# Gated retention outputs transposed by DMA on SyncE's queue instead of on TensorE

## The reference, cut to what matters

```python
proj = x @ w_in
q, k, v, g, cb, cc, cx, gr, gc = jnp.split(proj, SPLIT_IDX, axis=-1)
o, S = retention(q, k, v, S0, chunk_len)           # o: (B, L, 4 heads, 512), S carried from tile to tile
o = o * lax.rsqrt(jnp.mean(o * o, axis=-1, keepdims=True) + RMS_EPS)   # per-head norm
r = (jax.nn.silu(g) * o).astype(x.dtype) @ w_ret_out                   # 2048 -> 1024
m = jax.nn.sigmoid(gr) * r + jax.nn.sigmoid(gc) * c                    # c: the convolution's branch
h = layer_norm(DEEPNORM_ALPHA * x + m @ w_o, ln1_g, ln1_b)
```

## Time and profile before

| | |
|---|---|
| median of 3 runs | 1608.8 us |
| profiled execution, slowest core | 1608.5 us |
| span from first to last instruction in it | 1607.1 us (cores from 1603.9) |
| TensorE busy | 98% |
| VectorE, ScalarE, GpSimd busy | 50%, 29%, 17% |
| DMA engines: weights' queue, SyncE's queue | 59.2%, 9.2% |

### The profile page before, as it was taken

How to read it: one execution, slowest core, us unless ns; L and a number is a source line. 1 busy time by engine, 2 the same in 40 slices (tenths; PEclk the granted TensorE clock), 3 DMA queues, 4 the chain that set the end, 5 groups by cost and what they waited for, 6 DMA issues and landing times.

```text
span 1607.1 us, 27303 instructions; the slowest of 8 cores (1603.9 to 1607.1 us)
## 1 busy us (share of the span) xinstructions
PE 1570.0 (98%) x9196; PEld 874.3 (54%) x9288; DVE 798.9 (50%) x1469; ACT 468.2 (29%) x923; POOL 271.0 (17%) x504
## 2 busy tenths in 40 slices
PE   5999999999999999999999999999999999999997
PEld 2555566655664455555665566445555566556653
DVE  3566673255222856667424622275666852472226
ACT  1555511113110055552111311005555221131100
POOL 1122211012110322221101211022221110121102
PEclk9999999999999999999999999999999999999998
DMA  9955875569862698587565995369955877578621
GB/s 189 158 80 91 173 109 88 83 121 189 145 99 50 125 198 179 103 200 113 86 96 106 187 147 100 53 132 183 198 118 111 157 138 110 90 136 143 105 41 79
DMA packets 61382, 201.16 MB, mean 125 GB/s; under 512 B 6848, under 2 KB 8512, under 8 KB 61248
## 3 DMA queue, kind: packets, MB, share of 16 engines
q0 software_dynamic: 40752, 149.70, 59.2%
q1 hardware_dynamic: 19920, 48.66, 9.2%
q10 hardware_dynamic: 576, 1.05, 0.3%
HBM read 329.11 MB, written 19.96 MB: 217 GB/s over the span
## 4 chain that ended last, share of the span: by engine, by line
PE 90%; DVE 4%; issue 2%; DMA 2%; POOL 1%; DVEq 0%; ACTq 0%; POOLq 0%
PE P L906 21%; PE P L552 14%; PE P L720 11%; PE P L799 11%; PE P L938 9%; PE P L821 7%; PE P L517 7%; PE P L869 2%; PE P L674 2%; PE P L622 2%; DMA sb_W<-wb 1%; PE P L652 1%; PE P L618 1%; DVE sb_stat L844 1%; POOL sb_stat L848 1%
## 5 line engine op out<-in xcount | busy, mean ns | idle before, releaser
L906 PE MATMUL P<-sb_R,sb_W 128*128 128x384 bf16 x2112 | 345.7, 326 | 0.0
L906 PEld LDWEIGHTS P<-sb_R,sb_W 128*128 128x128 bf16 x2112 | 206.3, 98 | 136.0
L188 POOL DMA_DIRECT2D sb_W<-wb x278 | 153.3, 556 | 753.0 <-PE P L906 278.1
L552 PE MATMUL P<-sb_W,sb_xT 128*128 128x512 bf16 x1119 | 261.4, 379 | 3.1 <-DMA sb_W<-wb 1.0
L720 PE MATMUL P<-sb_xT,sb_W 128*128 128x384 bf16 x1152 | 196.0, 326 | 0.0
L552 PEld LDWEIGHTS P<-sb_W,sb_xT 128*128 128x128 bf16 x1152 | 110.6, 98 | 127.6 <-issue 4.2
L517 PE MATMUL P<-sb_xT,sb_W 128*128 128x384 bf16 x768 | 143.9, 333 | 16.4 <-ACT sb_xT L978 13.5
L720 PEld LDWEIGHTS P<-sb_xT,sb_W 128*128 128x128 bf16 x1152 | 110.9, 98 | 72.1 <-issue 1.2
L814 DVE TENSOR_TENSOR sb_scr<-P,sb_scr 128x384 f32<-128x384 f32 x96 | 53.5, 557 | 191.5 <-PE P L821 161.2
L911 ACT ACTIVATE sb_scr<-P 128x384 f32<-128x384 f32 x132 | 64.7, 490 | 247.9 <-PE P L906 247.9
L799 PE MATMUL P<-sb_xT,sb_W 128*128 128x384 bf16 x768 | 133.1, 326 | 0.0
(11 more groups left out here) (83 smaller groups left out, 1698.3 us busy)
## 6 DMA issues: line engine op xcount, KB each, us to landing
sb_W<-wb POOLq DMA_DIRECT2D x278, 512.0 KB, 10.3
sb_xres<-xp SPq DMA_DIRECT2D x16, 512.0 KB, 12.3
sb_xres<-sret SPq DMA_DIRECT2D x16, 512.0 KB, 15.5
yp<-sb_RA SPq DMA_DIRECT2D x16, 512.0 KB, 3.8
ss_o<-sb_xres SPq DMA_DIRECT2D x16, 512.0 KB, 9.2
sb_lnp<-lnp SPq DMA_DIRECT2D x12, 512.0 KB, 11.1
sb_xT<-xT POOLq DMA_DIRECT2D x5, 768.0 KB, 13.5
sb_cst<-cs SPq DMA_DIRECT2D x6, 384.0 KB, 8.6
```

Source lines behind the costliest of these rows:

```text
L188: self.E[q].dma_start(out=o, in_=i).then_inc(self.dsem[key], 16)
L552: S.pe([(lambda kc=kc: nc.tensor.matmul(P[b][:, :], xtile(s, kc, t), ws[kc // 4][:, kc % 4, :], start=(kc == 0), stop=(kc == 7)), [wc_(s, ...
L906: S.pe([(lambda kc=kc: nc.tensor.matmul(P[b][:, 0:n], w[:, kc, ji * 128:ji * 128 + 128], hT(kc, c0, c0 + n), start=(kc == 0), stop=(kc == 7)),
```

## The change

`og_tr` becomes one DMA transpose on SyncE's queue for each tile, from `og` straight into `goT`. `og` grows from two tiles to a ring of four, in a slot `so` that counts through all tiles of all heads; each slot has a semaphore (`gt0` to `gt3`). ScalarE's squares go into the slot that `gated` will write, so `junk` is gone. The scratch tiles shrink from 512 to 384 columns, the most that is used of them. The keys' transposes stay as they are.

```diff
-    def dma(self, q, key, pairs, reads=(), writes=()):
+    def dma(self, q, key, pairs, reads=(), writes=(), turn=False):
...
-            self.E[q].dma_start(out=o, in_=i).then_inc(self.dsem[key], 16)
+            (self.E[q].dma_start_transpose if turn else self.E[q].dma_start)(out=o, in_=i).then_inc(self.dsem[key], 16)
...
-        SCR = Reg("scr", 4 * 2048)
+        SCR = Reg("scr", 4 * 1536)
...
-        OG_ = Reg("og", 2 * 1024)
-        JK = Reg("junk", 1024)
+        OG_ = Reg("og", 4 * 1024)
...
-            S.op("act", lambda: nc.scalar.activation(out=junk(0), in_=P[b][:, :], func=AF.Square, accum_out=stat[:, c:c + 1]),
-                 reads=[f"P{b}"], writes=[junk.c(), sc(c)])
+            so = (h * NT + t) % 4
+            S.op("act", lambda: nc.scalar.activation(out=og(so), in_=P[b][:, :], func=AF.Square, accum_out=stat[:, c:c + 1]),
+                 reads=[f"P{b}"], writes=[og.c(so), sc(c)])
...
-                S.op("dve", lambda: nc.vector.scalar_tensor_tensor(out=og(t % 2), in0=P[b][:, :], scalar=stat[:, c + 1:c + 2],
+                S.op("dve", lambda: nc.vector.scalar_tensor_tensor(out=og(so), in0=P[b][:, :], scalar=stat[:, c + 1:c + 2],
...
         def og_tr(s, h, t):
-            b = bank()
-            pb = P[b][:].bitcast(BF16)
-            S.pe([(lambda ec=ec: nc.tensor.transpose(pb[:, ec * 128:(ec + 1) * 128], og(t % 2, ec * 128, ec * 128 + 128), idb(0)),
-                   [og.c(t % 2), idb.c()]) for ec in range(4)], [f"P{b}"])
+            so = (h * NT + t) % 4
             ci = chunk_of(s, t)
             o = t * 128 - CHUNKS[s][ci][0]
             tt = (o, o + 128)
             goT = goTc[s][ci]
-            S.op("act", lambda: nc.scalar.activation(out=goT((4 * h, 4 * h + 4), *tt), in_=pb[:, 0:512].rearrange("p (a b) -> p a b", a=4), func=AF.Copy),
-                 reads=[f"P{b}"], writes=[goT.c((4 * h, 4 * h + 4), *tt)])
-            rel(b)
+            S.dma("sp", f"gt{so}", [(goT((4 * h, 4 * h + 4), *tt), og(so))], reads=[og.c(so)], writes=[goT.c((4 * h, 4 * h + 4), *tt)], turn=True)
```

More of the change, by code:

```diff
@@ L353, in build_program @@
         cst = V3(CS, 0, 2, TS, F32)
-        scr = V3(SCR, 0, 4, 512, F32)
+        scr = V3(SCR, 0, 4, 384, F32)
         lnp = V3(LNP, 0, 2, 1024, F32)
@@ L360, in build_program @@
         sTm = V3(STM, 0, 2, 128, BF16)
-        og = V3(OG_, 0, 2, 512, BF16)
-        junk = V3(JK, 0, 1, 512, BF16)
+        og = V3(OG_, 0, 4, 512, BF16)
         hb = [V3(OG_, 0, 1, 1024, BF16), V3(GG, 0, 1, 1024, BF16), V3(SBF, 0, 1, 1024, BF16), V3(SBF, 2048, 1, 1024, BF16)]
@@ L642, in gated @@
             def gated():
-                S.op("dve", lambda: nc.vector.scalar_tensor_tensor(out=og(t % 2), in0=P[b][:, :], scalar=stat[:, c + 1:c + 2],
+                S.op("dve", lambda: nc.vector.scalar_tensor_tensor(out=og(so), in0=P[b][:, :], scalar=stat[:, c + 1:c + 2],
                                                                    in1=gg(t % 3), op0=ALU.mult, op1=ALU.mult),
-                     reads=[f"P{b}", sc(c + 1), gg.c(t % 3)], writes=[og.c(t % 2)])
+                     reads=[f"P{b}", sc(c + 1), gg.c(t % 3)], writes=[og.c(so)])
                 rel(b)
```

## The result

The changed kernel takes 1627.8 us (median of its runs, 1625.05 to 1630.07) against 1608.8 before: 1.0115 times as long, 95% interval 1.0103 to 1.0127: 1.2% slower, which is small, but far outside the scatter.

What follows compares the result with a forecast made beforehand. TensorE, busy 98% of the span, was taken to bound the kernel. 1608.5 − 16.3 saved + stalls of 21 and 21.6 + 2 × 1.5 for the slow clock = 1637.8, so 1637 us; range 1605 to 1690.

Steps and rivals of the forecast that it cites:

- Work taken away, 16.3 us: Output transposes on TensorE: 72 tiles at 0.226 us each come off the path, 16.3 us in all.
- A transpose lands in 3 us on an emptied queue: Each DMA transpose on SyncE's queue: 3 us from issue to landing when emptied, range 1 to 12 us.
- The upper bound, 12 us beside the weights: A DMA transpose's landing time if each of its pieces takes turns with a weight packet: 12 us.
- Where the wait strikes: Start of stages 1 and 2, head 0: tile 4's square waits for the first transpose, held behind two state loads.
- How long: TensorE's stalls in stages 1 and 2: 21 and 21.6 us, plus 1.5 us each for the slow clock.
- L = 621: Stage 1, head 0: the first transpose lands at 621 us, 3 us after the second load; bounds 608 and 634.
- Rival C: Stages 1 and 2: transpose not behind the loads' bytes, landing at 610, two 10 us stalls, 1612 us; chance 0.18.
- The slow clock, 1.5 us a stall: After each stall in stages 1 and 2, TensorE resumes at the 1.2 GHz level: 1.5 us added per stall.
- the 2 us for ScalarE's backlog: After TensorE resumes, some 2 us more lost while ScalarE works off value copies, a gate and a key copy.
- Stage 0, "no store stands in the queue": Stage 0: no store stands ahead in SyncE's queue, so no wait was priced there; waiting squares would mean error.
- Rival B: Transposes slow beside weights, 12 us each: longer stalls and some 5 us in stage 0, 1690 us; chance 0.20.
- Head 1 nothing, `ret_u` nothing: Head 1's repeated order priced at nothing (0 to 8 us a stage uncovered); last transposes have over 30 us before `ret_u`.

Runs made afterwards that it cites:

- late-load kernel: The changed kernel with the state loads for head h + 2 emitted after tile 4 instead of inside tile 0's update: 1.0186 times the kernel before (1.0104 to 1.0267).

## Why the prediction was right, and where it was not

1637 us were forecast with 1605 to 1690 as the range, and 1627.8 came: right in sign and within the range, 9 us too high. The steps, in its order:

- **Work taken away, 16.3 us: right to 0.1.** The undisturbed retention loops are 5.4 us shorter in each stage (196.5 and 201.2), 24 tiles of 0.225 us. The copies taken from ScalarE, the squares in the ring and the narrow scratch were priced at nothing; the other parts of the stages are 1.1 us longer in all (0.2, 0.2, 0.7), and no run tells which of them it is, if any.
- **A transpose lands in 3 us on an emptied queue: right.** The least was 2.4 us. But "a landing time of 2 to 5 us elsewhere" was too good: on core 2 the median of 72 was 7.3, the most 35.5. The upper bound, 12 us beside the weights, holds where they flow and nothing is blocked. The queues of core 2, 58 to 68 us:

```profile
q0 software_dynamic: 449, 1.63, 96.5%
q1 hardware_dynamic: 448, 0.11, 8.3%
```

  One piece of 256 bytes for each weight packet, 45 a us: 11 us for 512 pieces.
- **Where the wait strikes: right.** Square of tile 4, stages 1 and 2, released by the first transpose, which was issued just behind the second load (610.03, 610.61).
- **How long: the stall was 13.1 us each, not 21 + 1.5 and 21.6 + 1.5.** The step that failed is "those issued up to 599.1 land after at most 18.9 us, at 618 [...]. With the weights out of the way the second load lands at about 618, and the transpose 3 us later: L = 621". The clock of core 2 stands 4.8 us later here than in the trace before (stores at 579.11 against 574.30); the times in brackets are in that trace's time. The second load landed at 616.9 (612.1), 6 us sooner than said, and the transpose at 617.5 (612.7), 0.6 us behind it and not 3: its issue was long done when the load's last bytes went. On all cores, in both stages, the first transpose lands 0.6 to 0.7 us after the second load. In 612 to 622 us SyncE's queue, which until then had moved one packet for each of the weights', moved 2604 packets against their 96.
- **Why the weights ended sooner.** Their last block landed at 615.2 (610.4), where 618 was forecast. The forecast counted on three blocks, the third issued at 599.07. But GpSimd, which issues them, also works in order, and between the second block and the third it makes the factor of the norm of tile 4 (L636, L635 after), which needs the square. Core 6 before, then core 2 after:

```profile
595.49 1.16 POOL L188 DMA_DIRECT2D sb_W<-wb  x2 [2.77 <-PE P L582]
598.02 0.26 POOL L636 TENSOR_SCALAR sb_stat<-sb_stat,sb_vec 128x1 f32<-128x1 f32 x1 [1.37 <-ACT sb_junk L633]
599.07 0.62 POOL L188 DMA_DIRECT2D sb_W<-wb  x1
...
599.62 1.16 POOL L188 DMA_DIRECT2D sb_W<-wb  x2 [2.55 <-PE P L580]
618.48 0.26 POOL L635 TENSOR_SCALAR sb_stat<-sb_stat,sb_vec 128x1 f32<-128x1 f32 x1 [17.70 <-ACT sb_og L632]
619.44 0.62 POOL L188 DMA_DIRECT2D sb_W<-wb  x1
```

  So the waiting square itself held back the third block: GpSimd stood still from 600.8, TensorE only from 608.5. That block would have kept the weights flowing about 4 us longer (an estimate: before, it landed 3.8 us after the second, 617.9 against 614.2). Why the second, too, landed 3.8 us sooner than before stays open. A smaller slip has no weight: loads issued 7.3 us apart that both land after 15.6 us land 7.3 us apart, not 7.8.
- **The reason given for the stall was half of it.** "SyncE is held by the loads" is true, but the late-load kernel shows that without it the bytes ahead in the queue hold the transpose nearly as long (2 us of 13 won). Rival C gave L = 610 and a stall of 10 us, and by size alone the 13.1 us lie nearer to it than to the forecast. Its mechanism, that the transpose does not stand behind the loads' bytes, falls by the order of the landings above.
- **The slow clock, 1.5 us a stall: too small; the 2 us for ScalarE's backlog: too large.** After TensorE's idle piece of 10.5 us, the granted clock read 0.50, the 1.2 GHz level, through most of the next 5 us of work as well:

```profile
612.00:624.00 12.00, 4.58 (x11) 1.48 (x12) 3.54 (x7) 6.02 (x12) 2.49 (x5) 0.50 0.92 172
```

  From 619.0 to about 625 TensorE worked at half speed, which cost some 2.5 to 3 us (an estimate: half of that time). Its idle time in 604 to 640 us is 11.1 us, so only 0.6 us came on top of the 10.5. The two together are the 13.9 us that core 2 lost in stage 1 (215.1 − 201.2).
- **Stage 0, "no store stands in the queue", priced at nothing: wrong.** It cost 0 to 10.4 us by core, 10.4 on the slowest. The forecast named squares that wait in stage 0 as a sign that it was wrong, and they came. Rival B had 5 us there for slow pieces; what came is another mechanism, blocking by transposes in flight, that no row of before could show. It is the term that was missing.
- **Head 1 nothing, `ret_u` nothing: right** for this kernel; the second is not so with one in flight.

The two errors have opposite signs: 19 us too much for the two stalls with their clock, 10 on the slowest core too little. 1637.8 − 2 × (22.8 − 13.1) + 10.4 = 1628.8. Without stage 0's loss the same sum gives 1618, outside the forecast's own range of 1620 to 1655. So the closeness of the forecast is partly luck: the place and the cause of the two stalls were right, their length was not, and a loss that was not forecast made up half of the difference.

## What to carry to other kernels

Before work is moved from an engine to DMA, read what else stands in that queue at each place: all the bytes ahead, not only the instruction that holds the issuing engine, and the other queues that it takes turns with. Ask of an engine that will wait what else it issues or feeds: here the waiting square stopped GpSimd, and with it the weights. Move the work tile by tile: keep it where it was in the few places where the queue is full (here 18 of 72), and take the saving in the rest. On eight cores a disturbance that strikes one of them at random costs as much as one that strikes all.

## What the runs showed of the hardware

- A transposing DMA of 128x512 bf16, SBUF to SBUF, is 512 packets of 256 bytes and 32 of 4 bytes. SyncE needed 1.19 to 10.9 us to issue one on core 2 (median 1.29), and up to 17 us with eight in flight; its other transfers have a median of 0.38.
- Two queues that both have work take turns packet by packet, whatever a packet's size: 4 KB of weights for every 2 KB (1044 against 1040 packets in 29 us) or 256 bytes (449 against 448 in 10 us) of the other.
- Transposes in flight beside other busy transfers can block the DMA engines: 47 GB/s at a share of 1.31 for some 20 us, both queues slowed. The blocked slices of 10 us, in one profiled execution each: none with plain copies (ring of four or eight), 2 and 3 with one transpose in flight, 8 and 17 with two, 14 with four (20 and 31 with the late loads, with and without head 0's stores), 52 with eight; with head 0 on TensorE none with four and one with two. The count is no measure of the time: two in flight with 17 is faster than before, one in flight with 3 is slower. What exactly sets it off stays open: the number in flight and the crowding both count, and the places differ from core to core.
